# A hybrid encoder step on one core: 100 of 128 down tiles as three fp32r passes, low parts on GpSimd, queries in three groups, 12 row pairs moved to the up stage, gate factors on ScalarE

## The reference

```python
x = x + mixer(rmsnorm(x, norm1))                  # w_in: 1024 -> 9216, conv, retention, gates, w_out
x = x + peer(rmsnorm(x, norm2)); y = rmsnorm(x, final_g)

def blk(hb):                                      # PEER, a block of 128 tokens
    q = (hb @ w_q).reshape(128, 8, 2, 128)
    s = einsum('thpd,pkd->thpk', q, sub_keys)
    sv, si = top_k(s, 16)                         # of 128 keys, on both sides
    cand = sv[:, :, 0, :, None] + sv[:, :, 1, None, :]
    ts, tp = top_k(cand, 16)                      # 16 of 256; e = their expert numbers, of 16384
    g = softmax(ts)
    a = gelu(einsum('thkd,td->thk', u_tab[e], hb))
    return einsum('thk,thkd->td', g * a, v_tab[e])
```

## Time and profile before

| | us |
|---|---|
| median of three runs (lowest, highest) | 2370.47 (2367.83, 2370.59) |
| the profiled execution, whole | 2364.64 |
| its span | 2362.8 |
| TensorE busy in the span | 2288.3 (97%) |
| VectorE, ScalarE, GpSimd busy | 1595.8 (68%), 368.7 (16%), 789.0 (33%) |
| granted clock of TensorE, mean of the span | 0.988 |

### The profile page before, as it was taken

How to read it: one execution, slowest core, us unless ns; L and a number is a source line. 1 busy time by engine, 2 the same in 40 slices (tenths; PEclk the granted TensorE clock), 3 DMA queues, 4 the chain that set the end, 5 groups by cost and what they waited for, 6 DMA issues and landing times.

```text
span 2362.8 us, 27878 instructions
## 1 busy us (share of the span) xinstructions
PE 2288.3 (97%) x9545; PEld 1567.7 (66%) x9545; DVE 1595.8 (68%) x3138; ACT 368.7 (16%) x667; POOL 789.0 (33%) x606
## 2 busy tenths in 40 slices
PE   6999999899999999999999999999899999999998
PEld 5989889799997866655565656777544444444443
DVE  4476666467753175999888987989545655656556
ACT  3212213122222101111101111333100000000001
POOL 4222122123341003463544532101334544445440
PEclk9999999899999999999999999999999999999999
DMA  4998988989861337999999998878999999999995
GB/s 154 313 332 284 294 300 287 327 296 311 286 232 44 112 106 292 337 373 375 327 396 314 381 345 272 263 250 266 325 369 383 394 400 377 410 395 390 405 383 204
DMA packets 324120, 726.82 MB, mean 308 GB/s; under 512 B 30112, under 2 KB 179360, under 8 KB 324000
## 3 DMA queue, kind: packets, MB, share of 16 engines
q1 hardware_dynamic: 199776, 431.28, 51.5%
q0 software_dynamic: 73728, 268.47, 29.9%
q10 hardware_dynamic: 50496, 25.59, 3.6%
HBM read 595.65 MB, written 129.57 MB: 307 GB/s over the span
## 4 chain that ended last, share of the span: by engine, by line
PE 85%; DVE 7%; DMA 4%; issue 2%; SPq 1%; ACT 1%; POOL 0%; DVEq 0%; ACTq 0%; POOLq 0%
PE ps L1660 28%; PE ps L1616 27%; PE ps L1577 6%; PE ps L1395 5%; PE ps L1396 5%; PE ps L1397 5%; PE ps L1631 4%; DMA b<-in_u_t 3%; PE ps L1470 1%; DVE b L947 1%; PE ps L1460 1%; PE ps L1416 1%; PE ps L1602 1%; PE ps L1417 1%; PE ps L1418 1%
## 5 line engine op out<-in xcount | busy, mean ns | idle before, releaser
L1660 PE MATMUL ps<-b,b 128*128 128x512 f32 x1536 | 661.2, 593 | 7.3 <-ACT b L822 7.3
L1616 PE MATMUL ps<-b,b 128*128 128x384 f32 x2048 | 665.6, 486 | 0.0
L1616 PEld LDWEIGHTS ps<-b,b 128*128 128x128 f32 x2048 | 386.8, 190 | 263.4
L1660 PEld LDWEIGHTS ps<-b,b 128*128 128x128 f32 x1536 | 292.3, 190 | 376.0 <-issue 366.9
L621 POOL DMA_INDIRECT b<-u_rows,b x256 | 245.7, 960 | 846.0 <-DVE b L1271 604.1
L621 POOL DMA_INDIRECT b<-in_peer_v,b x256 | 335.8, 1312 | 167.0 <-DVE ps L1292 103.8
L1395 PE MATMUL ps<-b,b 128*128 128x320 f32 x1152 | 366.3, 318 | 5.0 <-ACT b L649 4.4
L1396 PE MATMUL ps<-b,b 128*128 128x320 f32 x1152 | 359.9, 312 | 0.0
L1397 PE MATMUL ps<-b,b 128*128 128x320 f32 x1152 | 359.8, 312 | 0.0
L586 POOL TENSOR_TENSOR b<-b,b 128x1024 fp32r<-128x1024 f32 x80 | 194.7, 2438 | 488.1 <-ACT b L634 483.6
L1292 DVE SCALAR_TENSOR_TENSOR ps<-b,b,ps 128x1024 f32<-128x1024 f32 x252 | 324.3, 1287 | 4.6
(11 more groups left out here) (147 smaller groups left out, 1760.7 us busy)
## 6 DMA issues: line engine op xcount, KB each, us to landing
b<-in_u_t SPq DMA_DIRECT2D x256, 512.0 KB, 6.1
u_rows<-b SPq DMA_DIRECT2D x512, 128.0 KB, 4.5
b<-in_peer_v SPq DMA_DIRECT2D x128, 512.0 KB, 8.3
b<-in_w_in SPq DMA_DIRECT2D x72, 512.0 KB, 5.8
acts<-b SPq DMA_DIRECT2D x128, 192.0 KB, 7.9
gates<-b ACTq DMA_DIRECT2D x12, 2048.0 KB, 8.0
b<-gates SPq DMA_DIRECT2D x32, 768.0 KB, 9.2
b<-acts SPq DMA_DIRECT2D x32, 768.0 KB, 15.4
```

The costliest lines, as they stand in the source:

```text
L1616: last = nc.tensor.matmul(ps[:, 2 + e % UP_BANKS, 0:TD], w[:, k * P:(k + 1) * P], h2[:, k, SD:T], start=(k == 0), stop=(k == KT - 1))
L1660: last = nc.tensor.matmul(ps[:, 2 + 2 * i + dh, :], p32[:, e % GROUP, i * P:(i + 1) * P], w[:, dh * 512:(dh + 1) * 512], start=(e == 0), s ...
```

## The change

1. **Down tiles.** 100 of the 128 (`three(e)`: e < 124 and e % 5 != 4) are done by `down_three`: 18 fp32r matmuls in place of 6 fp32 ones. ACT makes the high part of the weights and of p (`down_high`), POOL the low part of the weights (`low_of_tile`, 128 x 1024), DVE the low part of p (`low_of_gated`, 128 x 384). There are three buffers for high and low weights, so `down_high` and `low_of_tile` also wait until TensorE has finished the third such tile before. The final stage's buffers now share this space, and the load of `final_g` waits for it.
2. **Queries** in three groups, of 128, 128 and 384 tokens: 48 loads and passes of `w_q` tiles in place of 32; `scores(0)` stands behind the first group, `scores(1)` behind the first tile of the third.
3. **Pairs.** `GAP` is 10 in place of 6: 66 pairs around the retrievals and 56 beside the down tiles. The tables of places and `pair_at` have new numbers. POOL's row fetches of the down stage now stand between the low parts.
4. **Gate factors.** ACT does the product with the gate factor too: behind each Gelu it waits for it and makes two products of 128 x 1. DVE's L1283 falls away.

```diff
+QUERY_TOKENS = (slice(0, P), slice(P, SD), slice(SD, T))
-EXP_AT = {1: 12, 2: 40, 3: 67, 4: 95}
-SCORES_AT = {2: 8, 3: 49, 4: 77}
-PICKT_AT = {2: 46, 3: 74, 4: 101}
+EXP_AT = {1: 6, 2: 36, 3: 65, 4: 95}
+SCORES_AT = {2: 2, 3: 45, 4: 75}
+PICKT_AT = {2: 42, 3: 72, 4: 101}
-GAP = 6
+GAP = 10
-    e = 27.4 * turn + (-3.3 + 2.35 * (i + 0.3) if i < INSIDE else 17.4 + 1.04 * (i - INSIDE))
+    e = 29.9 * turn + (-9.8 + 2.28 * i if i < INSIDE else 9.9 + 1.01 * (i - INSIDE))
     return max(0, int(e))
+def three(e):
+    return e < NKEY - GROUP and e % 5 != 4
...
+            def low_of_tile(e):
+                n = SPLIT[e]
+                pool.wait_ge(v_high, n + 1)
+                if n >= 3:
+                    pool.wait_ge(a_used, A_V + THREES[n - 3] + 1)
+                nc.gpsimd.tensor_tensor(v_lo[n % 3][:, :], raw[:, e % GROUP, :], v_hi[n % 3][:, :].bitcast(F32),
+                                        ALU.subtract).then_inc(v_split, 1)
...
+            for e in range(NKEY):
+                if three(e):
+                    low_of_tile(e)
+                while n < len(ORDER) and pair_after(freed_after(n)) < e:
+                    row_fetch(n)
+                    n += 1
...
             def pair_gelu(b):
                 act.wait_ge(dot_one, PAIR * (b + 1))
-                nc.scalar.activation(acted[:, b % LINES, :], dots[:, b % LINES, :], ACT.Gelu).then_inc(act_done, 1)
+                nc.scalar.activation(acted[:, b % LINES, :], dots[:, b % LINES, :], ACT.Gelu).then_inc(gelu_done, 1)
+                act.wait_ge(gelu_done, b + 1)
+                if b >= LINES:
+                    act.wait_ge(row_done, PAIR * (b - LINES + 1))
+                for i in range(PAIR):
+                    r_ = b * PAIR + i
+                    last = nc.scalar.activation(row_w[:, b % LINES, i:i + 1], acted[:, b % LINES, i:i + 1], ACT.Copy,
+                                                scale=row_g[:, r_ // P, r_ % P:r_ % P + 1])
+                last.then_inc(act_done, 1)
...
+            def down_high(e):
...
+                act.wait_ge(loaded[i % GROUP], 16 * ((N_WQ + i) // GROUP + 1))
+                nc.scalar.activation(v_hi[n % 3][:, :], raw[:, e % GROUP, :], ACT.Copy).then_inc(v_high, 1)
+                act.wait_ge(p_ready, e + 1)
+                nc.scalar.activation(p_hi[:, e % GROUP, :], p32[:, e % GROUP, :], ACT.Copy).then_inc(p_high, 1)
...
             for e in range(NKEY):
                 weigh(e)
-                while b < NPAIR_U + (NPAIR - NPAIR_U) * (e + 1) // NKEY:
+                if e and three(e - 1):
+                    low_of_gated(e - 1)
+                while b < NPAIR and pair_after(b) == e:
                     pair_step(b)
                     b += 1
...
+            def down_three(e, i):
+                u, n = e % GROUP, SPLIT[e] % 3
+                tok = slice(i * P, (i + 1) * P)
+                for dh in range(2):
+                    out, cols = ps[:, 2 + 2 * i + dh, :], slice(dh * 512, (dh + 1) * 512)
+                    nc.tensor.matmul(out, p_hi[:, u, tok], v_hi[n][:, cols], start=(e == 0), stop=False)
+                    nc.tensor.matmul(out, p_hi[:, u, tok], v_lo[n][:, cols], start=False, stop=False)
+                    last = nc.tensor.matmul(out, p_lo[:, u, tok], v_hi[n][:, cols], start=False, stop=False)
+                return last
```

105 lines of the change are left out of this document (76 added, 29 removed).

## The result

The changed kernel takes **2415.9 us** (median; 2412.8 to 2424.3), the one before 2370.5 in the same session: a ratio of 1.020, 95% interval 1.017 to 1.023. It is slower by 45 us. The forecast was 2362 and its range ended at 2412. The third rival had named 2418.

The account below looks back on a forecast made before the run. TensorE was taken to bound the up and down stages. Down -34, queries +1.9 and up +24 us gave -8 on the profiled 2364.6, so 2356.6, or 2362 as a median; range 2318 to 2412.

Parts of the forecast that it names:

- The third rival: Down stage: subtractions block the port, clock falls; 21.3 us a group, whole 2418; decides from 19.8 a group; chance 0.25.
- Queries, +1.9: Query matmuls: 256 of 0.223 us in place of 128 of 0.432, so +1.9 us.
- The 12 pairs at no cost: Up stage: 12 more pairs, 56 us of VectorE's work less 66 x 0.2, fit beside TensorE's work.
- The early stall, +24: Up stage: TensorE waits 11 us at `scores(2)` and 5 at tile 4, each with clock loss; +24 us, ends 14 and 32.
- Entry, +2: Start of the down stage: the first tile waits for high and low parts made one after the other, +2 us.
- TensorE's own time for a three-pass tile: Down stage: 18 fp32r matmuls take 4.20 us in place of 5.17; 97 us less over 100 tiles.
- half of one wait in the route is 1 us: Down stage: VectorE's two-SBUF-operand work waits while GpSimd subtracts; 1 us a group.
- the 19.5 us for a group: Down stage: four tiles take 19.5 us, ends 17.9 and 22.8; stage 627 us in place of 661.
- My routes: Down stage, two routes to TensorE's next group: weights 19.0 to 20 us, gated activations 18.0 or 19.6.
- the floor: Down stage: 7.34 MB at 395 GB/s, 18.6 us for the mean group if this rate is the DMA engines' limit.
- the main case: The forecast's own case: groups of 18.9 to 20.2 us, whole 2343 to 2384 us; chance 0.42.
- The signs I had named: Profile: `weigh` 1.2 or more, port; dot above 1.3, two-input rule; landings near 12, the main case, near 16, the third rival.

Follow-up runs that it names:

- with the stall out: ScalarE's step of the first pairs placed among the query groups, against the changed kernel: 2389.3 us, ratio 1.008.
- the run with the short subtraction: GpSimd's subtraction on 128 of 1,024 columns from the fourth three-pass tile on, against the changed kernel: 2379.7 us, ratio 1.005.
- the square: Down stages of four kernels: changed kernel 676 us; low part of p before next weighing 669; GpSimd's subtraction on 128 of 1,024 columns 635; both 600.

## Why the prediction was wrong, point by point

Summed against the profiled execution, the forecast was 2356.6 and the execution took 2417.0: 60 us.

- **Queries, +1.9:** a little short. From the first query matmul to the first up matmul it took 152.5 us in place of 148.4, 4.1 more, and 3.0 more with the stall out; four waits of 0.3 to 0.8 us, 2.0 in all where one of 0.6 stood, are most of the rest.
- **The 12 pairs at no cost:** right. With the stall out the up stage, from its first matmul to its last, takes 759.1 us, as before.
- **The early stall, +24:** right in its place, its two waits and its size, 26.7 by the run without it. Nothing gave it back.
- **The mixing stage** ended 3.7 us later than in the profile of before (first query matmul at 781.5 and 777.8 us), in code that is the same. In the profiles of three experiments it is 774.6, 783.0 and 784.3, so I take this for scatter.
- **Entry, +2:** 3.9 (waits of 11.1 to 11.3 us where 7.3 stood). The low parts of the first tile cost nearly twice what I took.
- **TensorE's own time for a three-pass tile,** 4.20: right, near 4.1 in the run with the short subtraction.
- **The step that failed is the price of the port, "half of one wait in the route is 1 us", and with it the 19.5 us for a group.** A group measured: (676 - 20.7)/31 = 21.1 us with everything, (600 - 20.7)/31 = 18.7 with the subtraction short and the order changed. So the two causes hold 2.4 us a group where I had 1, and the rest of the group is 18.7 where the 19.5 leaves 18.5: (1.4 + 0.2) x 31 is some 50 us, the bulk of the error (676 against 625). By the square, the exclusion alone is 36 to 64 us of the 75, 1.2 to 2.1 us a group, and the order 11 to 38. The term was sized from one wait of 2.79 us. It missed that GpSimd has two subtractions in a row after its fetches, so that one operation waits 5.5 us; that the dots wait and block as well; and that the low part stands in VectorE's row behind a weighing that waits for a transfer. This last I had written down as a route, with the activations' landing in it, but not as something that the exclusion would make longer.
- **The 19.5 wasn't the sum of its own terms either.** My routes gave 19.0 to 20 for the weights and 18.0 or 19.6 for the activations, and the 1 us came on top of both. The later route decides, so a group should have been 20.0 us or more, which is past the 19.8 from which the change loses. With its terms added as they stand the forecast would have had the right direction.
- **What is left without both is near what I took for the floor.** 18.7 us a group, against 18.6 for 7.34 MB at 395 GB/s. That this is the transfers' limit isn't shown: the measured rate is 372, and TensorE still waits 26.5 us for low parts and 3.3 for weights in that run.
- **The clock.** I had put its losses at the up stage alone. In the down stage behind its entry the records show it at half sixteen times, 58 us together, which is up to 29 us of TensorE's work; the third rival had this part and the main case had not.
- **The signs I had named** decided in part as I said. A `weigh` of 1.2 or more would speak for the port: 1.27. A dot above 1.3 would show the rule on two inputs: 1.42. Landings near 16 were to mark rival 3: they were 10.2 us on average. That sign was wrong, since the transfers had become quicker and the waits were elsewhere. The waits at the tiles 4g + 3 and 4g were to hold the rest; they are 36 of 84 us, and 28 and 21 stand at 4g + 1 and 4g + 2.
- **The chance.** The third rival had 0.25 and came within 2 us of the median (2418). Its mechanism was the right one, but that the sum fits so well is in part luck: it left out the order, its down stage without the entry was 681 us where 676 was measured, and everything ahead of it took 37 us more than before where it had 28. What spoke for it stood in the rows: 3.1 subtractions a group against 0.56 us operations that feed TensorE directly, and a clock that had fallen behind each long wait. Its deciding point was 19.8 us a group; I had put the main case 0.3 us below it, and gave it the largest chance although my ends were 17.9 and 22.8.

The Trainium skill ("SBUF — State Buffer", Who interferes with whom) says that a VectorE instruction with two SBUF inputs and a GpSimd instruction that reads SBUF exclude each other, while one with at most one SBUF input, outside VectorE's two-port modes, doesn't contend. The trace agrees: dots from 1.22 to 1.42 and up to a mean of 1.71, row sums unchanged at 1.28. It also says that whoever issues first holds the ports for the whole instruction. The row above, where a VectorE operation that started 0.44 us earlier ended behind two subtractions, shows another outcome, with a row fetch under way at its start.

## What to carry to other kernels

When work is moved from TensorE to engines that feed it, sum the new operations on the route to TensorE's next tile, and not only their busy time: here VectorE was busy 559 of 676 us and GpSimd 480, and TensorE waited for both. Do as much of a split as the cover allows: 60 tiles, each beside a plain one, gave 47 us, while 100 lost 9 against none at all. Before a request is moved up in a queue, look at what it waits for, how much it carries, and whose data stands right behind it.
